# A decoder trunk of float32 weights: the low halves of the hidden rows from a product with minus the identity, and rows added at the end

## The reference

```python
def moe_swiglu(h, w_router, w_gate, w_up, w_down):
    ...
    top_v, top_e = lax.top_k(logits, TOP_K)
    gates = jax.nn.softmax(top_v, axis=-1)
    ...
    def expert_block(args):
        xb, e = args
        return (jax.nn.silu(xb @ w_gate[e]) * (xb @ w_up[e])) @ w_down[e]
    ...
    y = yb.reshape(P, D)[dest] * g_sorted[:, None].astype(t.dtype)
    out = jax.ops.segment_sum(y, tok_sorted, num_segments=N)
```

## Time and profile before

| | us |
| --- | --- |
| median of 3 runs | 1455.68 (1454.31 to 1455.74) |
| the profiled execution | 1454.98 |
| its span, first to last instruction | 1453.5 |
| TensorE busy | 1403.7 (97%) |
| VectorE busy | 1207.9 (83%) |
| ScalarE busy | 1001.9 (69%) |
| GpSimd busy | 122.4 (8%) |

### The profile page before, as it was taken

How to read it: one execution, slowest core, us unless ns; L and a number is a source line. 1 busy time by engine, 2 the same in 40 slices (tenths; PEclk the granted TensorE clock), 3 DMA queues, 4 the chain that set the end, 5 groups by cost and what they waited for, 6 DMA issues and landing times.

```text
span 1453.5 us, 19359 instructions
## 1 busy us (share of the span) xinstructions
PE 1403.7 (97%) x6739; PEld 1155.7 (80%) x6739; DVE 1207.9 (83%) x1504; ACT 1001.9 (69%) x1280; POOL 122.4 (8%) x185
## 2 busy tenths in 40 slices
PE   8999999999999999999999999999999999999967
PEld 6768888888988888888888788888888778787745
DVE  7776554544887689999999999999999989998947
ACT  7556444444632577888888877888888878887835
POOL 1000400000243065000000000000000000000010
PEclk9999999999999999999999999999999999999979
DMA  9515797554543459999999999999999999999971
GB/s 335 188 59 172 276 412 275 185 180 156 175 145 117 159 195 394 391 413 407 395 413 407 413 393 407 402 395 409 410 396 409 409 388 412 408 414 404 409 267 75
DMA packets 135743, 460.33 MB, mean 317 GB/s; under 512 B 9192, under 2 KB 18464, under 8 KB 121312
## 3 DMA queue, kind: packets, MB, share of 16 engines
q1 hardware_dynamic: 126752, 433.09, 77.7%
q0 software_dynamic: 7168, 25.43, 4.8%
q10 hardware_dynamic: 1728, 0.59, 0.2%
HBM read 438.37 MB, written 20.71 MB: 316 GB/s over the span
## 4 chain that ended last, share of the span: by engine, by line
PE 67%; DVE 13%; DMA 7%; issue 4%; ACT 3%; POOL 0%; DVEq 0%; ACTq 0%; SPq 0%; POOLq 0%
PE bank L1795 19%; PE bank L1797 19%; PE bank L1796 19%; DVE w_lo L1161 5%; DVE w_lo L1156 5%; DMA raw<-in_w_up_moe_dram 3%; DMA raw<-in_w_gate_moe_dram 2%; PE bank L1801 2%; PE bank L1802 2%; PE bank L2000 1%; ACT w_hi L742 1%; PE bank L2175 1%; DMA raw<-in_w_down_moe_dram 1%; ACT w_hi L747 1%; DVE t_hi L1658 1%
## 5 line engine op out<-in xcount | busy, mean ns | idle before, releaser
L742 ACT ACTIVATE w_hi<-raw 128x1024 fp32r<-128x1024 f32 x411 | 436.3, 1062 | 374.3 <-PE bank L1797 329.0
L1156 DVE TENSOR_TENSOR w_lo<-raw,w_hi 128x1024 fp32r<-128x1024 f32 x411 | 503.3, 1225 | 152.7 <-ACT w_hi L742 150.1
L1161 DVE TENSOR_TENSOR w_lo<-raw,w_hi 128x1024 fp32r<-128x1024 f32 x411 | 504.4, 1227 | 0.6 <-ACT w_hi L747 0.6
L1795 PE MATMUL bank<-w_hi,t_hi 128*128 128x512 f32 (+1 forms) x1088 | 430.5, 396 | 3.4 <-DVE w_lo L1156 2.0
L747 ACT ACTIVATE w_hi<-raw 128x1024 fp32r<-128x1024 f32 x411 | 430.4, 1047 | 0.8 <-DMA raw<-in_w_in_attn_dram 0.8
L1796 PE MATMUL bank<-w_lo,t_hi 128*128 128x512 f32 (+1 forms) x1088 | 421.7, 388 | 0.0
L1797 PE MATMUL bank<-w_hi,t_hi 128*128 128x512 f32 x672 | 262.3, 390 | 0.0
L1795 PEld LDWEIGHTS bank<-w_hi,t_hi 128*128 128x128 f32 x1088 | 204.9, 188 | 46.2 <-issue 3.7
L1796 PEld LDWEIGHTS bank<-w_lo,t_hi 128*128 128x128 f32 x1088 | 204.7, 188 | 40.8 <-issue 1.0
L1795 PE MATMUL bank<-w_hi,h_hi 128*128 128x512 f32 x408 | 165.2, 405 | 20.5 <-DVE w_lo L1156 13.8
L1797 PE MATMUL bank<-w_hi,t_lo 128*128 128x512 f32 (+1 forms) x472 | 182.4, 386 | 0.0
(11 more groups left out here) (345 smaller groups left out, 1342.5 us busy)
## 6 DMA issues: line engine op xcount, KB each, us to landing
raw<-in_w_gate_moe_dram SPq DMA_DIRECT2D x112, 1024.0 KB, 12.6
raw<-in_w_up_moe_dram SPq DMA_DIRECT2D x112, 1024.0 KB, 12.4
raw<-in_w_down_moe_dram SPq DMA_DIRECT2D x112, 1024.0 KB, 12.6
raw<-in_w_in_rec_dram SPq DMA_DIRECT2D x16, 1024.0 KB, 5.7
raw<-in_w_gate_dense_dram SPq DMA_DIRECT2D x14, 1024.0 KB, 5.2
raw<-in_w_up_dense_dram SPq DMA_DIRECT2D x14, 1024.0 KB, 5.3
raw<-in_w_down_dense_dram SPq DMA_DIRECT2D x14, 1024.0 KB, 5.0
raw<-in_w_in_attn_dram SPq DMA_DIRECT2D x8, 1024.0 KB, 14.8
```

Of the source, the lines that this page charges most:

```text
L742: act.activation(w_hi[:, (u - 1) % SPL, half], raw[:, r, half], ACT.Copy).then_inc(hi_half, 1)
L1156: dve.tensor_tensor(w_lo[:, s, half], raw[:, r, half], w_hi[:, s, half].bitcast(F32), ALU.subtract).then_inc(lo_half, 1)
L1161: dve.tensor_tensor(w_lo[:, s, half], raw[:, r, half], w_hi[:, s, half].bitcast(F32), ALU.subtract).then_inc(lo_done, 1)
L1795: pe.matmul(o, lh, rh, start=start, stop=False)
```

## The change

1. In large rounds the remainder is no longer VectorE's. The transposes leave the bank's sum open (`closed=False`); ScalarE copies it to `h_hi` as before; TensorE multiplies `h_hi` by minus the identity (`minus`) into the same bank (`take_rounded`), which leaves the remainder there; ScalarE copies that to `h_lo` and frees the bank (`hidden_end`), after a wait for `rest_done`.
2. The gain of the norm is applied once, by GpSimd, to the rows before they are sent (`gain_row`, a DMA of 512 KB in ScalarE's queue, and two products of 128x1024). `gather_hi` and `gather_lo` are then two instructions of 128x512 each instead of eight.
3. Both halves of a round's results are copied by ScalarE (`results`).
4. The last down collects in GATE + 1 and UP + 1 (banks 1 and 3, `YLAST`) instead of YB and YB + 1.
5. The four additions of fetched rows to `X` stand behind the last split instead of between the splits.

The diff, cut to its core (a line "..." stands for lines left out):

```diff
@@ -569,7 +573,11 @@
...
             pool.wait_ge(rows_set, 1)
-            pool.wait_ge(u_done, TT)
+            pool.wait_ge(gain_row_in, 16)
+            for t in range(TT):
+                pool.wait_ge(u_done, TT + t)
+                pool.tensor_tensor(U[:, t, :], U[:, t, :], gain_row, ALU.mult).then_inc(u_done, 1)
+            pool.wait_ge(u_done, 2 * TT)
             pool.wait_ge(y_stored, 16)
@@ -976,22 +984,28 @@
...
             saw(0, 1)
+            act.activation(minus[:], ident[:], ACT.Copy, scale=-1.0).then_inc(minus_set, 1)
             split_to(U0 + AHEAD)
+            act.dma_start(gain_row, g_ffn[1:2, :].broadcast_to([P, D])).then_inc(gain_row_in, 16)
             act.dma_start(gf[:], g_final.rearrange("(o n) -> o n", o=1).broadcast_to([P, D])).then_inc(gf_in, 16)
...
+            for m, b in enumerate((GATE + 1, UP + 1)):
+                wait_full(b)
+                for c in range(4):
+                    k = 4 * m + c
+                    act.activation(t_hi[:, k, 0:CAP], bank[b][:, c * P:(c + 1) * P], ACT.Copy,
+                                   scale=col[:, 24 + k:25 + k]).then_inc(th_done, 1)
             def gather_hi(rows_t):
...
                     wait_full(b)
-                    for c in range(4):
-                        k = 4 * m + c
-                        act.activation(rows_t[:, k, 0:CAP], bank[b][:, c * P:(c + 1) * P], ACT.Copy,
-                                       scale=col[:, 24 + k:25 + k]).then_inc(th_done, 1)
-            gather_hi(t_hi)
+                    act.activation(rows_t[:, 4 * m:4 * m + 4, 0:CAP], bank[b][:].rearrange("p (c n) -> p c n", c=4),
+                                   ACT.Copy).then_inc(th_done, 1)
             assert (n.count[f"fill{YB}"], n.count[f"fill{YB + 1}"]) == Y_FREED
@@ -1013,29 +1027,47 @@
...
                     hidden_beside(g)
-                    split_to(to + 2)
+                else:
+                    hidden_hi(g)
+            def hidden_end(g, small):
+                if small:
+                    split_to(start + group_at(g) + SPL + 2)
                     hidden_hi_small(g)
                 else:
-                    hidden_hi(g)
-            def left_results():
+                    split_to(start + behind_pair(2 * g + 1) + SPL)
+                    act.wait_ge(rest_done, n.step("rest"))
+                    act.activation(h_lo[:, g % 2, :], bank[TR + g % 2][:], ACT.Copy).then_inc(free[TR + g % 2], 1)
+            def results():
...
                 wait_units(start + FFN_UNITS, YB, YB + 1)
-                act.activation(ybuf[:, 0:BLK], bank[YB][:], ACT.Copy).then_inc(free[YB], 1)
+                for m in range(2):
+                    act.activation(ybuf[:, m * BLK:(m + 1) * BLK], bank[YB + m][:], ACT.Copy).then_inc(free[YB + m], 1)
                 n.count["half"] = 2 * (start + AHEAD)
...
                 for w in range(WIDE + 1):
+                    hidden(2 * w, small)
                     if w == 0:
-                        hidden(0, small)
+                        if small:
+                            hidden_end(0, small)
+                        gate_rows(0, start + behind_pair(1))
+                        if not small:
+                            hidden_end(0, small)
                         hidden(1, small)
+                        hidden_end(1, small)
                     elif w < WIDE:
-                        hidden(2 * w, small)
-                    gate_rows(w, start + behind_pair(4 * w + 1 if w < WIDE else 4 * w))
-                    if w:
-                        hidden(2 * w + 1 if w < WIDE else 2 * w, small)
+                        gate_rows(w, start + behind_pair(4 * w + 1))
+                        hidden_end(2 * w, small)
+                        hidden(2 * w + 1, small)
+                        hidden_end(2 * w + 1, small)
+                    else:
+                        gate_rows(w, start + behind_pair(4 * w))
+                        hidden_end(2 * w, small)
                     if last and w == 1:
@@ -1649,18 +1681,25 @@
...
+            for m, b in enumerate((GATE + 1, UP + 1)):
+                wait_full(b)
+                dve.wait_ge(th_done, n.step("th", 4))
+                for c in range(4):
+                    k = 4 * m + c
+                    ins = dve.scalar_tensor_tensor(
+                        t_hi[:, k, CAP:2 * CAP], bank[b][:, c * P:(c + 1) * P], col[:, 24 + k:25 + k],
+                        t_hi[:, k, 0:CAP].bitcast(F32), ALU.mult, ALU.subtract)
+                ins.then_inc(free[b], 1)
             def gather_lo(rows_t):
                 for m, b in enumerate((GATE + 1, UP + 1)):
                     wait_full(b)
-                    dve.wait_ge(th_done, n.step("th", 4))
-                    for c in range(4):
-                        k = 4 * m + c
-                        ins = dve.scalar_tensor_tensor(
-                            rows_t[:, k, CAP:2 * CAP], bank[b][:, c * P:(c + 1) * P], col[:, 24 + k:25 + k],
-                            rows_t[:, k, 0:CAP].bitcast(F32), ALU.mult, ALU.subtract)
-                    ins.then_inc(free[b], 1)
-            gather_lo(t_hi)
+                    dve.wait_ge(th_done, n.step("th"))
+                    dve.tensor_tensor(rows_t[:, 4 * m:4 * m + 4, CAP:2 * CAP],
+                                      bank[b][:].rearrange("p (c n) -> p c n", c=4),
+                                      rows_t[:, 4 * m:4 * m + 4, 0:CAP].bitcast(F32), ALU.subtract).then_inc(free[b], 1)
             split_to(U0 + AHEAD)
@@ -1729,19 +1763,18 @@
...
                 hidden_lo(g + 1)
-                if g == 2:
-                    dve.wait_ge(y_back, 16 * 2 * TT)
-                if g < 6:
-                    r, t = (g - 2) // 2, g % 2
+            split_to(start + DOWN)
+            dve.wait_ge(y_back, 16 * 2 * TT)
+            for r in range(2):
+                for t in range(TT):
                     link(dve.scalar_tensor_tensor(X[:, t, :], back[t][r], row_f[:, 3, t, r:r + 1], X[:, t, :],
                                                   ALU.mult, ALU.add))
-            split_to(start + DOWN)
             dve.wait_ge(last_done, TT + 1)
-            saw_product(YB, YB + 1)
-            for m in range(2):
+            saw_product(*YLAST)
+            for m, b in enumerate(YLAST):
                 dve.wait_ge(yh_done, m + 1)
-                dve.tensor_tensor(y_lo[m], bank[YB + m][:].rearrange("p (c n) -> p c n", c=4), y_hi[m].bitcast(F32),
-                                  ALU.subtract).then_inc(free[YB + m], 1)
+                dve.tensor_tensor(y_lo[m], bank[b][:].rearrange("p (c n) -> p c n", c=4), y_hi[m].bitcast(F32),
+                                  ALU.subtract).then_inc(free[b], 1)
             for m in range(2):
@@ -2019,7 +2057,14 @@
...
-            def down_unit(j, small=False, into=0):
+            def take_rounded(g):
+                pe.wait_ge(hh_done, n.step("hh"))
+                b = TR + g % 2
+                pe.matmul(bank[b][:], minus[:], h_hi[:, g % 2, :], start=False, stop=True,
+                          skip_group_check=True).then_inc(rest_done, 1)
+            def down_unit(j, small=False, into=0, to=(YB, YB + 1)):
@@ -2324,8 +2369,13 @@
...
                 for at in range(2 * FB):
+                    if at % 2 == 0 and at > 1:
+                        if small_down:
+                            n.step("hh")
+                        else:
+                            take_rounded(at // 2 - 1)
                     if at % 4 < 2 and at // 4 * 2 + at % 2 < FB:
-                        expert_transposes(at // 4 * 2 + at % 2)
+                        expert_transposes(at // 4 * 2 + at % 2, closed=small_down)
                     block_pair(at, rows_t, small_next)
@@ -2364,10 +2420,10 @@
...
             expert_transposes(1, into=1)
-            open_bank(YB)
-            open_bank(YB + 1)
+            for b in YLAST:
+                open_bank(b)
             for j in range(DOWN - 1):
-                down_unit(j, into=1)
+                down_unit(j, into=1, to=YLAST)
                 if j % 2 and j // 2 + 2 < FB:
```

More of the change, by code:

```diff
@@ L1683, in hidden @@
                 else:
[L1684 to L1691 removed]
+                    saw(TR + g % 2)
+                    n.step("hh")
             def phase(small, last=False):
@@ L1706, in phase @@
                 split_to(start + FFN_UNITS + AHEAD)
-                right_results()
+                saw_product(YB, YB + 1)
+                n.count["half"] = 2 * (start + AHEAD)
             for w in range(WIDE):
@@ L2036, in down_unit @@
                         if small:
-                            last = pair(bank[YB + m][:], h_hi[:, hp, hs], w_hi[:, s, ws], w_lo[:, s, ws], first, fin)
+                            last = pair(bank[to[m]][:], h_hi[:, hp, hs], w_hi[:, s, ws], w_lo[:, s, ws], first, fin)
                         else:
-                            last = triple(bank[YB + m][:], h_hi[:, hp, hs], h_lo[:, hp, hs], w_hi[:, s, ws],
```

(13 more changed lines are left out.)

38 lines of the change are left out of this document (21 added, 17 removed).

## The result

The changed kernel takes 1437.65 us (median of 4 runs, 1436.39 to 1438.75), the kernel before 1455.52 beside it. The ratio is 0.9879, with a 95% interval from 0.9862 to 0.9896. The forecast was 1436.8 within 1427 to 1444. The profiled run took 1438.75, with a span of 1437.2; before these were 1454.98 and 1453.5.

What follows compares the result with a forecast made beforehand. It took the memory stream to bound the rounds up to the last loads. Last down -20.15, additions +1.1, queue +0.5: -18.55 against 1454.98, so 1436.4; 1436.8 for the median, range 1427 to 1444 for 8 in 10.

Steps and rivals of the forecast that it cites:

- The last down: The kernel's last products: length 41.0 us instead of 55.9, 14.9 less; with the earlier start, an end 20.15 us earlier.
- Its start: First product of the last down at 1381.5 us instead of 1386.75, 5.25 less.
- ahead of the rounds: Before the rounds: GpSimd's two gain products, 5.7 us, fit into its 30.22 us wait; `minus` also counts 0.
- "uncovered" price: Ahead of the rounds: what GpSimd's two gain products would cost if its wait did not hide them, 5.7 us.
- The tail: Behind the last down's products: the additions of fetched rows end later, costing 1.1 us more.
- The rounds: Rounds up to the last loads: bound by the stream, so engine work saved or added counts 0, with one exception.
- dry queue: Round from 824 to 941: TensorE is always busy, its added products may empty the load queue; 0.5 us, bounds 0 and 1.6.
- The fetched rows: At the kernel's end: they land at 1408 to 1413 us, ahead of 1418; each us beyond 1418 would cost one.
- Rival A: VectorE sets the pace in the rounds, so they shed 30 us: about 1407; chance 0.09.
- Rival B: Large rounds: the engines' lag sets the pace, TensorE's 28 added products cost 6.4 us: about 1443; chance 0.14.
- Rival C: Large rounds: TensorE waits for the new `rest_done` handover with ScalarE, making it slower, up to 1512; chance 0.04.
- Rival D: At the end: fetched rows land later than the last down's products, the wait only moves: about 1455; chance 0.03.

Runs made afterwards that it cites:

- e1: The changed kernel without its part 2 (no gain row, no GpSimd products; the scaled copies and remainders are back): 1436.01 us, ratio 0.9873.
- e3: The changed kernel without its part 1 (VectorE subtracts the remainders of large rounds again; TensorE's products and ScalarE's copy of the remainder go): 1437.76 us.
- e12: e11 with part 1 undone too, so VectorE subtracts the remainders of the large rounds: 1432.70 us.
- e8: e1 with ScalarE's copy `ST` in the last round moved ahead of the split and rounding of group 3: 1433.13 us, ratio 0.9847.
- e11: e8 with VectorE asked for the last up rows one split earlier in the last round, which left every engine's order unchanged: 1432.73 us.
- e4: The changed kernel without its parts 4 and 5 (old banks for the last down, additions and their wait between the splits): 1457.05 us, ratio 1.0012.
- e10: e9 together with e3's edit (halved expert loads, VectorE subtracts the remainders of large rounds; output not the reference's): 1424.98 us.
- e6: The changed kernel without its part 5 alone (additions of fetched rows and their wait between the last splits again): 1458.73 us.
- e2: e1 with the gain row loaded and two GpSimd products of the same size behind the four sends, results unread: 1438.12 us.
- e7: The changed kernel with expert loads behind the first expert's gate and up units filling 64 of 128 partitions (output not the reference's): 1432.86 us.
- e9: e7 with another half: those expert loads bring half the columns of all 128 partitions (output not the reference's): 1430.02 us.
- e5: The changed kernel without its part 4 alone (last down summed in YB and YB + 1 again): 1441.05 us.

## Why the prediction was right, and where not

The mechanism held. Nearly all of the gain is in the last down, and the rounds give none.

- **The last down.** Its length was forecast at 41.0 us and is 1425.88 - 1385.04 = 40.84. The way there was right as well: an undisturbed pair from one row, two pairs without transposes, and no stop.
- **Its start** was forecast at 1381.5 and is 1385.04. The step that failed is "ahead of the rounds": I laid GpSimd's 5.7 us beside its own idle time of 30 us and asked who waits for GpSimd. Nobody did. But its products slowed two of VectorE's splits by 3.8 us and made the sends 7 us later; TensorE stopped for it, the memory brought 1.3 MB less up to 720 us, and none of it came back later (the lag on e1 is 2.2 us at the first store and 2.3 at the last round's begin): some 2.2 us of the 3.5 by seven traces, 1.1 to 1.6 by e1's median. The "uncovered" price of 5.7 would have held it. The rest I can't assign: e3 and e12 take part 1 out and don't give it back, and e8 and e11, whose instructions stand in the same order, differ by 1.5 us at the same store.
- **The tail.** Forecast +1.1. It takes 1437.2 - 1425.88 = 11.3 us from the end of the products, before 1453.5 - 1442.65 = 10.85: +0.5. `y_lo` came 0.7 behind the products; I had 0.9. But the row behind it moved from 1.44 to 1.98 only, since both halves now run back to back.
- **The rounds.** The forecast's one exception to "counts 0", 0.5 us for a dry queue in the round from 824 to 941, had the right mechanism, but it holds in two rounds, at 1.5 and 1.7 us, and nothing of it is left at the end: the median of e3 is 0.1 us from the changed kernel's.
- **Together:** 3.5 more for the start, 0.2 less for the length, 0.6 less for the tail and the 0.5 of the dry queue, which is part of the 3.5: 1436.4 + 2.2 = 1438.6, against 1438.75 in the profiled run. That the forecast of the median came within 0.9 is in part luck: I put the median 0.4 above the profiled run, and it is 1.1 below it. From profile to profile the forecast was 2.3 us short.
- **The fetched rows.** I expected their landing at 1408 to 1413; it was 1416 to 1417. ScalarE's copies came at 1386.26 with the late rounds, GpSimd's chain began at 1389.45 where I had about 1384.5, and it took 27 us instead of 23.5. There was room for it.
- **Rival A** is refuted: e3, e4, and above all e10, where VectorE has the remainders, the loads are early, and TensorE still waits only 3.0 us for its splits in all the rounds. The estimate from the Trainium skill's 425 GB/s ("HBM Reference", section Specifications (TRN2)) left room for A; 412 is the highest of the stretches of rounds shown after the change.
- **Rival B** named a true cost in the wrong place: the products do cost TensorE 5 us, but only where the stream isn't the bound; with all bytes they cost 3.2 us in two rounds, which the stream takes away again.
- **Rival C:** ScalarE waited 3.3 us in all for `rest_done`, in five places, the longest 0.9, and I had said about 1.
- **Rival D** is what e6 is: with the wait left where it was, the landing of the rows sets the end.

## What to carry to other kernels

Work moved off an engine that isn't the bound is worth nothing, however busy that engine looks; halve the bytes of the stream for one run, over all partitions, and it shows who is next and by how much. Work put on an idle engine is free only if it doesn't slow a neighbour: ask what the neighbour does in those microseconds, not only who waits for the idle one. A wait for a transfer belongs behind the last piece of work that others need; taking away what stands ahead of the wait is worth nothing until that is done.

## What the runs showed of the hardware

- A GpSimd product (128x1024, two inputs in SBUF) and VectorE's subtraction of two SBUF inputs did not run at the same time. The two products ended at about 540.4 and 543.67 (6.61 us for both from 537.06), and the two slow subtractions at 541.42 and 544.77: each 1.1 us behind a product's end, nearly its own full length. VectorE waited for the whole product. In e2 the second product ended at 548.49 and the slow half at 549.57, again 1.1 us behind. The Trainium skill has this rule ("SBUF — State Buffer", section SBUF: two separate sides: one engine gets the port pair for its whole instruction, and the other is blocked); the trace agrees, and I had not weighed it in the forecast.
- Loads of 0.5 MiB over 64 partitions (e7) moved 204 to 221 GB/s at a DMA share of 0.96 to 1.03, and landed in 9.1 to 10.5 us. The same bytes over 128 partitions (e9) moved 197 to 216 GB/s at a share of 0.65 to 0.74, and landed in 3.9 to 4.5. So a DMA share near 1 stood once for 404 GB/s (the changed kernel) and once for half of it.
- A stop of TensorE doesn't always bring the same stretch at half clock. From the end of the stop for `ST` to the last transposes of the last round it took 54.92 us in e1; 56.46, 56.51, 56.46, 56.45 and 56.41 in the kernel before, the changed kernel, e2, e4 and e5; and 57.72 in e3 and e6. The stops were 2.74 to 2.75 us, in e3 3.00; the mean granted clock from 1324 to 1335 us was 1.00 in e1, 0.84 in the changed kernel and 0.69 in e3. A difference of 1.6 or even 2.8 us between two single profiles can be that alone. The four runs of the changed kernel show the like: 1436.39 and 1436.67 us at a mean granted clock of 0.999, 1438.63 and 1438.75 at 0.997.
